# Causal differential attention: a second buffer for the first score map, its bias pass two tiles ahead, and the branch projections dealt to other tile steps

## The reference

```
s = einsum('bqhcd,bkhcd->bhcqk', qi, k) * scale + bias      # c = 0, 1: two score maps
s = where(rel >= 0, s, -1e30);  p = softmax(s)
a = p[:, :, 0] - lam * p[:, :, 1];  o = einsum('bhqk,bkhd->bqhd', a, v)
merged = g_a * (y_a @ proj_a) + g_b * (y_b @ proj_b) + g_c * (y_c @ proj_c)
```

## Time and profile before

| | us |
|---|---|
| median of 3 runs | 2671.74 |
| lowest, highest | 2671.67, 2676.66 |
| the profiled execution | 2672.17 |
| its span in the trace | 2670.3 |
| TensorE busy | 2551.3 |
| VectorE busy | 1373.5 |
| ScalarE busy | 697.1 |
| GpSimd busy | 659.5 |

### The profile page before, as it was taken

One profiled execution on the slowest core, in us unless ns is written; L12 is line 12 of the kernel. 1 busy time (PEld: TensorE's weight loads), 2 busy tenths in 40 slices (PEclk: granted clock), 3 DMA queues, 4 the chain that ended last, 5 costly groups with the idle time before them and its releaser, 6 DMA issues.

```text
span 2670.3 us, 32753 instructions
## 1 busy us (share of the span) xinstructions
PE 2551.3 (96%) x12342; PEld 2098.6 (79%) x12342; DVE 1373.5 (51%) x1770; ACT 697.1 (26%) x989; POOL 659.5 (25%) x368
## 2 busy tenths in 40 slices
PE   7998989999999999999999989999999999899997
PEld 4877767777788788888888867888888887688875
DVE  5646573644554552255225664357777764534344
ACT  3222222222211111001000122155566651222111
POOL 1322322222233333333333322210100003222221
PEclk9999999999999999999999989999999999899998
DMA  4133342421422111111121111100000002111111
GB/s 158 45 98 126 111 134 103 134 87 48 158 71 71 40 53 49 47 47 47 47 64 53 50 56 32 47 25 9 8 16 8 8 9 59 38 31 33 38 40 71
DMA packets 44733, 158.16 MB, mean 59 GB/s; under 512 B 5452, under 2 KB 6732, under 8 KB 44526
## 3 DMA queue, kind: packets, MB, share of 16 engines
q1 hardware_dynamic: 38172, 132.94, 16.2%
q10 hardware_dynamic: 6482, 24.12, 2.5%
HBM read 143.67 MB, written 13.37 MB: 59 GB/s over the span
## 4 chain that ended last, share of the span: by engine, by line
PE 87%; DVE 9%; issue 3%; ACT 1%; DVEq 0%; DMA 0%; ACTq 0%; SPq 0%
PE PS L549 67%; PE PS L995 3%; PE PS L928 3%; PE PS L934 2%; PE PS L967 2%; PE PS L685 1%; PE PS L590 1%; PE PS L582 1%; DVE cols L2161 1%; PE PS L918 1%; DVE H L1672 1%; DVE SC L1829 1%; PE PS L720 1%; PE PS L1084 1%; PE PS L711 1%
## 5 line engine op out<-in xcount | busy, mean ns | idle before, releaser
L549 PE MATMUL PS<-H,w_hl 128*128 128x512 f32 x6624 | 1554.5, 395 | 46.5 <-DVE H L1672 17.8
L549 PEld LDWEIGHTS PS<-H,w_hl 128*128 128x128 f32 x6624 | 1250.1, 190 | 333.3 <-issue 46.6
L524 POOL CAST w_hl<-w_raw 128x1024 fp32r<-128x1024 f32 x180 | 197.3, 1096 | 1936.1 <-PE PS L549 1545.8
L526 POOL TENSOR_TENSOR w_hl<-w_raw,w_hl 128x1024 fp32r<-128x1024 f32 x180 | 453.4, 2519 | 14.4
L549 PE MATMUL PS<-FF,w_hl 128*128 128x512 f32 x1056 | 239.8, 389 | 0.0
L549 PEld LDWEIGHTS PS<-FF,w_hl 128*128 128x128 f32 x1056 | 198.3, 188 | 41.1
L928 PE MATMUL PS<-CKV,QN 128*128 128x512 f32 (+1 forms) x576 | 142.0, 364 | 0.0
L1398 ACT ACTIVATE SC<-SC,vec 128x1024 f32<-128x1024 f32 x22 | 25.4, 1153 | 392.5 <-DVE SC L2027 392.4
L995 PE MATMUL PS<-PT,CKT 128*128 128x256 f32 x960 | 120.7, 283 | 1.5 <-DVE PT L2177 1.5
L995 PEld LDWEIGHTS PS<-PT,CKT 128*128 128x128 f32 x960 | 117.7, 191 | 2.4 <-DVE PT L2177 1.7
L2177 DVE TENSOR_TENSOR PT<-PS,PT 128x512 fp32r<-128x512 f32 (+1 forms) x192 | 103.6, 596 | 22.9 <-ACT PT L1494 22.4
(11 more groups left out here) (289 smaller groups left out, 2398.5 us busy)
## 6 DMA issues: line engine op xcount, KB each, us to landing
w_raw<-in_units SPq DMA_DIRECT2D x182, 512.0 KB, 3.6
AW<-in_ada SPq DMA_DIRECT2D x48, 512.0 KB, 3.7
X<-in_x SPq DMA_DIRECT2D x8, 512.0 KB, 7.7
SC<-in_x ACTq DMA_DIRECT2D x8, 512.0 KB, 3.7
out<-X ACTq DMA_DIRECT2D x8, 512.0 KB, 3.1
m_part<-GTA ACTq DMA_DIRECT2D x7, 512.0 KB, 5.1
M<-m_part SPq DMA_DIRECT2D x7, 512.0 KB, 8.5
g_part<-GTB ACTq DMA_DIRECT2D x6, 512.0 KB, 2.6
```

What stands on the lines that cost most here:

```text
L524: pool.tensor_copy(hi_part, raw).then_inc(w_hi, 1)
L526: pool.tensor_tensor(lo_part, raw, hi_part.bitcast(F32), ALU.subtract).then_inc(w_split, 1)
L549: mm = pe.matmul(PS[:, out_at + a:out_at + a + m], w(s, wp, w0 + k), src[:, o:o + m], start=(k == 0 and wp == 0 and xp == 0), stop=(k == k ...
```

## The change

SA becomes two tiles, `[SA, SQ]`, used in turn. `biased`, `exps` and `combine` run two tiles ahead: within step t they serve tile t+2, and `head_start` does tile 1 as well. Each engine's order in a step changes with it. VectorE now does its part of slot (t, 0), waits for weigh(t) and copies it, then `biased(t+2)`, its part of slot (t, 1), a modulation tile, `combine(t+2)`, and the "out" modulation tile. ScalarE does AT(t), slot (t, 0) (from t = 1), `exps(t+2)`, slot (t, 1). TensorE's order within a step is as before.

The deal changes from two places per step to explicit counts. In heads 1 and 2 step 0 has ga half 0 at (0, 0), and ga half 1 and gb half 0 at (0, 1); from there every piece stands one place earlier, so the steps read: step 1 gb | pa, step 2 pb | gc, step 3 gc | ga, step 4 ga | gb, step 5 gb | pa, step 6 pb | gc, step 7 gc. Head 0 starts with gb half 0 at (0, 1) and nothing at (0, 0). The last head has ga | ga, gb, gb, pa | pb, ga, ga | gb, gb | pa, pb over steps 0 to 7, and its gc pieces are put around the two steps of the normalisation. Modulation tiles get other places: none at "bias" in steps 6 and 7 and in the steps with pb, one more at "out" in step 3, and a start at step 1 of head 0 rather than step 2.

```diff
             blocks = half_units(a) + half_units(b)
+            counts = [(1, 1), (1, 0), (1, 0), (1, 1), (1, 0), (1, 1), (1, 1), (1, 0)]
         else:
             blocks = half_units(a) + both("gc", a) + half_units(b) + both("gc", b)
+            counts = [(1, 2)] + [(1, 1)] * 6 + [(1, 0)]
         if h == 0:
             blocks = blocks[2:]
-        free = [(t, n) for t in range(QT_N - last) for n in range(2)]
-        for place in [(5, 1), (4, 1) if last else (7, 1)][:len(free) - len(blocks)]:
-            free.remove(place)
+            counts[0] = (0, 1)
...
-        here = [("bias", t) for t in range(QT_N - 1)] + [("out", t) for t in range(QT_N)]
+        here = [("bias", t) for t in range(QT_N - 2) if t not in weighed] + [("out", t) for t in range(QT_N)]
+        here += [("out", t + 1) for t in weighed if t + 1 < QT_N - 2]
...
-    SA = at("SA", T, X_AT)
+    SA = [at("SA", T, X_AT), SQ]
...
-                if t + 1 < QT_N:
-                    exps(h, t + 1)
                 if t:
                     slot(h, t, 0)
+                if t + 2 < QT_N:
+                    exps(h, t + 2)
                 slot(h, t, 1)
...
-                if t + 1 < QT_N:
-                    v.wait_ge(done[1], before("diff", 1) + 17 * h + 2 + 2 * t)
-                    biased(h, t + 1)
-                    slot(h, t, 0)
-                    ada_at(h, t, "bias")
-                    combine(h, t + 1)
+                slot(h, t, 0)
                 v.wait_ge(done[1], before("diff", 1) + 17 * h + 3 + 2 * t)
                 chain(v.tensor_copy(OC[:, t * P:(t + 1) * P], PS[:, 1024:1024 + P]))
...
+                if t + 2 < QT_N:
+                    biased(h, t + 2)
+                slot(h, t, 1)
+                ada_at(h, t, "bias")
+                if t + 2 < QT_N:
+                    combine(h, t + 2)
                 ada_at(h, t, "out")
-                if t + 1 == QT_N:
-                    slot(h, t, 0)
-                slot(h, t, 1)
```

More of the change, by code:

```diff
@@ L127, in head_slots @@
         a, b = 2 * h, 2 * h + 1
-        last = h == HEADS_C - 1
-        if last:
+        if h == HEADS_C - 1:
             blocks = half_units(a) + half_units(b)
+            counts = [(1, 1), (1, 0), (1, 0), (1, 1), (1, 0), (1, 1), (1, 1), (1, 0)]
         else:
             blocks = half_units(a) + both("gc", a) + half_units(b) + both("gc", b)
+            counts = [(1, 2)] + [(1, 1)] * 6 + [(1, 0)]
         if h == 0:
             blocks = blocks[2:]
-        free = [(t, n) for t in range(QT_N - last) for n in range(2)]
-        for place in [(5, 1), (4, 1) if last else (7, 1)][:len(free) - len(blocks)]:
-            free.remove(place)
-        assert len(free) == len(blocks), (h, len(free), len(blocks))
-        slots.append(dict(zip(free, blocks)))
+            counts[0] = (0, 1)
+        here = {}
+        for t, pair in enumerate(counts):
+            for n, count in enumerate(pair):
+                here[t, n] = sum(blocks[:count], [])
+                blocks = blocks[count:]
+        assert not blocks
+        slots.append(here)
     return slots
@@ L150, in ada_places @@
     for h in range(HEADS_C - 1):
-        here = [("bias", t) for t in range(QT_N - 1)] + [("out", t) for t in range(QT_N)]
+        weighed = [t for t in range(QT_N) if any(kind == "pb" for s in range(2) for kind, _, _ in SLOTS[h].get((t, s), []))]
+        here = [("bias", t) for t in range(QT_N - 2) if t not in weighed] + [("out", t) for t in range(QT_N)]
+        here += [("out", t + 1) for t in weighed if t + 1 < QT_N - 2]
         here = sorted((t, place) for place, t in here) + [(QT_N, "norm")] * 2 + [(QT_N, "start")]
         for t, place in here:
-            if h == 0 and t < 2 or h == HEADS_C - 2 and place == "start" or n == ADA_TILES:
+            if h == 0 and t < 1 or h == HEADS_C - 2 and place == "start" or n == ADA_TILES:
                 continue
@@ L496, in _ @@
         sp.wait_ge(oc_ready, QT_N * HEADS_C)
+        sp.wait_ge(mp_ready, KC)
         for c in range(KC - 1):
@@ L710, in turn_weights @@
             for kb in range(t + 1):
-                mm = pe.transpose(PS[:, 1024 + kb * P:1024 + (kb + 1) * P], SA[:, kb * P:(kb + 1) * P], ident[:, :])
+                mm = pe.transpose(PS[:, 1024 + kb * P:1024 + (kb + 1) * P], SA[t % 2][:, kb * P:(kb + 1) * P], ident[:, :])
             mm.then_inc(done[1], 1)
@@ L729, in diff_head @@
                 slot(h, t, 1 if t == 0 else 0)
-                if h == HEADS_C - 1 and t == QT_N - 1:
-                    dense("gc", KC - 2, 0)
                 weigh_values(h, t)
@@ L737, in diff_head @@
             if h == HEADS_C - 1:
+                dense("gc", KC - 2, 0)
+                norm_sum(h + before("diff", "norm"), h * 9 + (b("diff", 2) + 8))
                 dense("gc", KC - 2, 1)
-            else:
-                dense("q", h + 1, 0)
-                dense("q", h + 1, 1)
+                dense("gc", KC - 1, 0)
+                norm_spread(h + before("diff", "norm"), h * 9 + (b("diff", 3) + 8))
+                dense("gc", KC - 1, 1)
+                return
+            dense("q", h + 1, 0)
+            dense("q", h + 1, 1)
             norm_sum(h + before("diff", "norm"), h * 9 + (b("diff", 2) + 8))
             for half in range(2):
[L744 to L747, removed]
+                dense("k", h + 1, half)
             norm_spread(h + before("diff", "norm"), h * 9 + (b("diff", 3) + 8))
@@ L1257, in exps @@
             act.wait_ge(neg_ready, h * 8 + (t + 1))
-            for c, S in enumerate((SA, SB)):
+            for c, S in enumerate((SA[t % 2], SB)):
                 o = 2 * (t % 2) + c
@@ L1270, in head_start @@
             act.sem_inc(free[1], 1)
+            exps(h, 1)
         def diff_head(h):
@@ L1281, in diff_head @@
                 act.sem_inc(free[1], 1)
-                if t + 1 < QT_N:
-                    exps(h, t + 1)
-                if t + 2 == QT_N and not last:
-                    load_bias(h + 1)
                 if t:
                     slot(h, t, 0)
+                if t + 2 < QT_N:
+                    exps(h, t + 2)
+                if t + 3 == QT_N and not last:
+                    load_bias(h + 1)
                 slot(h, t, 1)
@@ L1292, in diff_head @@
                     act.activation(CC[:, :], CC[:, :], ACT.Silu).then_inc(c_silu, 1)
+            act.wait_ge(oc_ready, h * 8 + 8)
+            act.activation(ACC, OC, ACT.Square).then_inc(acc_ready, 1)
             if last:
                 gate_out("gc", KC - 2, 0)
[L1296 to L1302, removed]
-            norm(h + before("diff", "norm"), QT_N)
[L1304 to L1308, removed]
+            else:
+                queries_keys(h + 1, "q", 0)
+                queries_keys(h + 1, "q", 1)
+            norm(h + before("diff", "norm"), QT_N)
+            if last:
+                gate_out("gc", KC - 2, 1)
+                gate_out("gc", KC - 1, 0)
+            else:
+                queries_keys(h + 1, "k", 0)
+                queries_keys(h + 1, "k", 1)
             act.wait_ge(xt, h + (xts[0] + 1))
             act.activation(OCS[:, h * T:(h + 1) * T], TMP0, ACT.Copy).then_inc(hi, 1)
-            if not last:
+            if last:
+                gate_out("gc", KC - 1, 1)
+            else:
                 head_start(h + 1)
@@ L1796, in combine @@
             o = 2 * (t % 2)
-            S0, S1 = SA, SB
+            S0, S1 = SA[t % 2], SB
             v.wait_ge(exp_ready, h * 16 + (2 * t + 2))
@@ L1842, in ada_at @@
                     v.wait_ge(c_silu, 2)
-                ada(k, ACC if place == "norm" else SQ)
+                ada(k, ACC if place == "norm" else SQ if place == "start" else TMP0)
         def diff_head(h):
             for t in range(QT_N):
-                if t + 1 < QT_N:
-                    v.wait_ge(done[1], before("diff", 1) + 17 * h + 2 + 2 * t)
-                    biased(h, t + 1)
-                    slot(h, t, 0)
-                    ada_at(h, t, "bias")
-                    combine(h, t + 1)
+                slot(h, t, 0)
                 v.wait_ge(done[1], before("diff", 1) + 17 * h + 3 + 2 * t)
@@ L1879, in head_start @@
             ada_at(h - 1, QT_N, "start")
+            biased(h, 1)
+            combine(h, 1)
         v.sem_inc(ada_used, 2)
```

## The result

The changed kernel takes 2683.4 us (median of five, 2682.8 to 2688.8) against 2671.7; the ratio is 1.0049 with an interval of 1.0037 to 1.0061. It is slower, by 11.7 us, and 2681 was forecast. The spans of the two profiled executions differ by as much: 2680.7 against 2670.3, 10.4 us.

The account below looks back on a forecast made before the run. TensorE, busy 2551 of 2670 us, was taken as the bound. New waits of 36.9 us against 32.1 (4.8 more) plus 4.7 for the clock made 9.5 us more: 2681 us, forecast's own range 2675 to 2688, 8-in-10 range 2662 to 2691.

Parts of the forecast that it names:

- Step 0 of heads 1 and 2: ScalarE drains ga half 1 only after exps(2), so gb half 1 waits: 3.7 us per head, 7.4 in all.
- pb after pa: pb half 0 needs pa half 0 weighted, behind biased(t+2): 1.3 us at tile 7, plus 1.8 in all for tile 3.
- The race at tile 3: VectorE's negation against GpSimd's subtraction: no wait at pb if the negation is first, otherwise 1.9 us; half taken, 1.8 in all.
- gc after pb: gc half 0 needs pb half 0 weighted, which stands behind modulation tiles and combine(t+2) on VectorE: waits of 20.55 us together.
- Head 0: turn(0) waits 1.4 us for the pair VC is copied from, weigh(1) 1.85 us for AT(1): together 3.25 us.
- In the last head, which has no modulation tiles, I find no wait left: TensorE in the last head: no waits remain after the change, so that head gains all of its 5.2 us.
- The clock: TensorE's clock falls after seven of the long waits, 2.34 us each: 16.4 us against 11.7 before, 4.7 more.
- the eight waits that the prediction names: New TensorE waits or pairs of 2.2 us or longer, six of them 3.5 or more; seven were counted as clock falls.
- The modulation loads held nothing up, as supposed: Modulation tile loads, tightest in step 3: landing 5 us after issue, a load comes when used; any lateness costs under 1 us.

Follow-up runs that it names:

- The run with the reduction: The changed kernel with the negation of the two maxima done by a reduction with negate instead of a multiply by -1: 2674.2 us, ratio to before 1.0003.

## Why the prediction was right

The time and its sign came out as forecast, and outside the last head nearly every wait with its place, its releaser and its size; that the total fits so closely is partly luck (below). (Measured: the idle time with its 0.14 us of overlap.)

- *Step 0 of heads 1 and 2*: 3.7 us each forecast, 3.67 measured, and shown by itself: without it 11.4 us less, where 10.5 were expected.
- *pb after pa*: 1.3 us in step 6 forecast, 1.34 to 1.41 measured. The race at tile 3, which I had put at even, was lost in all three heads: 1.8 us each. It cost 1.9 us more than the half that I took. The run with the reduction shows that the held negation was the cause.
- *gc after pb*: in step 6 2.3, 3.55 and 4.85 forecast, 2.25, 3.54 and 4.79 measured. In step 2, with the race lost, the working gives some 3.5, 2.9 and 1.6; measured 3.58, 2.96 and 1.69. The run with the tiles behind pb shows it.
- *Head 0*: 1.4 and 1.85 forecast, 1.39 and 1.92 measured.
- *"In the last head, which has no modulation tiles, I find no wait left"* was wrong. Its waits are 4.7 us with the overlap, where the kernel before has 4.9 by the same rows (4.1 of idle time in six waits; the 5.2 of the prediction is 0.3 too much). I had looked at pb and at the normalisation, and not at what `exps(4)`, issued a step ahead, does to AT(3) behind it when pa opens its unit 0.4 us after scores(4):

```profile
641.22 3.02 PE L557 MATMUL PS<-YA,w_hl 128*128 128x512 f32 x12
...
643.16 2.23 DVE L1800 TENSOR_SCALAR cols<-cols 128x2 f32<-128x2 f32 x1
645.43 0.83 ACT L1268 ACTIVATE SA<-SA,cols 128x640 f32<-128x640 f32 x1 [5.71 <-DVE cols L1800]
...
647.07 0.57 ACT L1288 ACTIVATE AT<-PS 128x512 f32<-128x512 f32 x1
```

- *The clock* was mis-sized: seven falls at 2.34 us, 4.7 us more than before, were forecast; it was six at 1.5 to 2.5, 10.5 us together and 1.2 less than before. Five came at the eight waits that the prediction names, all of them at 3.4 us and over; the sixth stands in the last head. The granted clock was 0.98 in heads 1 and 2, where 0.95 had been expected.

Waits: 4.8 us more forecast, 11.6 measured, of which the last head is 4.7 and the race 1.9. Clock: 4.7 more forecast, 1.2 less measured. The two errors of six to seven us had opposite signs, so that the total of 9.5 against 10.4 is better than its parts: that is luck. The modulation loads held nothing up, as supposed: VectorE never waits for one in the heads of the changed kernel.

## What to carry to other kernels

Running a stage further ahead moves its instructions in front of others in each in-order queue. Go through every queue for what now stands behind it, and ask of each such instruction whether the bound engine waits for it; here a handful of small edits, and no more buffers, turned a change that lost 12 us into one that wins 37. Filler work (the modulation tiles) belongs behind the instruction that frees a resource for the bound engine, not just anywhere with enough slack on the average. Count an instruction at its held duration where another engine's long one starts by a fixed trigger near it, and see that the data of moved filler work has landed at its new place.

## What the runs showed of the hardware

A VectorE instruction that touches none of GpSimd's data can be stretched many times over while GpSimd's 128x1024 instructions run: 0.17 to 2.2 us for two elements, 0.16 to 2.4 for one, 1.22 to 3.4 for a multiply of a tile (shortest and longest over all runs). GpSimd's own were stretched in turn, the subtraction from 2.4 to 3.5 us and the cast before it from 1.04 to 2.1. The hold lies inside the duration of the instruction and does not show as idle time before it.

In these traces the clock after a wait is not settled by the length of the wait. After 2.11 us it stayed up in the changed kernel, and after 2.08 in the same place it fell in the run with other counts in the last head:

```profile
252.96 7.34 PE L557 MATMUL PS<-H,w_hl 128*128 128x512 f32 x24 [2.08 <-DVE GTB L1821]
```

After 2.82 us it stayed up in the changed kernel and fell in the run with the drains first:

```profile
343.85 7.33 PE L557 MATMUL PS<-H,w_hl 128*128 128x512 f32 x24 [2.82 <-DVE GTB L1824]
```

In the run with one tile ahead and the new dealing both happened in one execution: in step 7 of head 1 the gate piece after a wait of 3.07 us took 7.32 us, in step 7 of head 2 the one after 3.06 took 5.71. Single executions show no more than that a fall can come or stay away: over the 20 executions of the kernel before in one group the mean granted clock ran from 0.978 to 0.983.

After every wait of 3.4 us and over in the changed kernel and the runs built on it the clock had fallen, at 1.4 to 2.9 us of slower matmuls. What decides below that stays open.
